# The down product of a SwiGLU block by Strassen's seven products, with the combinations of h formed in the gate and up tiles

## What is computed

```python
h = _rmsnorm(x, norm2_g)
ff = silu(einsum('btd,df->btf', h, w_gate)) * einsum('btd,df->btf', h, w_up)
return x + einsum('btf,fd->btd', ff, w_down)
```

## Time and profile before

| | us |
|---|---|
| median of 3 runs | 2161.58 (2156.37 to 2165.09) |
| the profiled execution | 2164.21 |
| its span | 2162.4 |
| TensorE busy | 2122.7 (98%) |
| gate and up tiles | about 1454 to 1898 |
| down product | about 1898 to 2154 |

### The profile page before, as it was taken

One profiled execution on the slowest core, in us unless ns is written; L12 is line 12 of the kernel. 1 busy time (PEld: TensorE's weight loads), 2 busy tenths in 40 slices (PEclk: granted clock), 3 DMA queues, 4 the chain that ended last, 5 costly groups with the idle time before them and its releaser, 6 DMA issues.

```text
span 2162.4 us, 36192 instructions
## 1 busy us (share of the span) xinstructions
PE 2122.7 (98%) x14248; PEld 1981.8 (92%) x14248; DVE 1070.9 (50%) x2112; ACT 632.3 (29%) x1354; POOL 723.7 (33%) x636
## 2 busy tenths in 40 slices
PE   7999999999999999999999999999999999999999
PEld 6788899999877778999989999999999999999998
DVE  5565777775233331333266544498554554452222
ACT  5221365535233232333221011133232322221001
POOL 3423320232212222222042434324444444554310
PEclk9999999999999999999999999999999999999999
DMA  6625534454548744555457551414545545387612
GB/s 196 211 84 190 175 108 148 134 183 164 184 152 296 263 139 148 163 149 161 119 194 264 181 175 61 152 62 159 202 143 179 186 147 178 105 326 291 258 44 79
DMA packets 233736, 365.17 MB, mean 169 GB/s; under 512 B 39223, under 2 KB 134263, under 8 KB 230871
## 3 DMA queue, kind: packets, MB, share of 16 engines
q1 hardware_dynamic: 211534, 317.48, 44.3%
q10 hardware_dynamic: 22032, 45.38, 6.0%
HBM read 276.19 MB, written 174.68 MB: 209 GB/s over the span
## 4 chain that ended last, share of the span: by engine, by line
PE 55%; DVE 4%; issue 1%; DMA 1%; ACT 0%; DVEq 0%; ACTq 0%
PE ps L2855 24%; PE ps L2199 17%; PE ps L366 4%; PE ps L367 4%; PE ps L368 4%; PE ps L1637 1%; DMA h_mem<-c_ht 1%; PE ps L1412 0%; DVE x_c L2549 0%; DVE x_a L2549 0%; PE ps L1629 0%; PE ps L1620 0%; PE ps L1646 0%; PE ps L3498 0%; DMA rw<-hm_t 0%
## 5 line engine op out<-in xcount | busy, mean ns | idle before, releaser
L341 POOL CAST whi<-raw 128x512 fp32r<-128x512 f32 x228 | 174.6, 766 | 1048.1 <-PE ps L682 429.4
L343 POOL TENSOR_TENSOR wlo<-raw,whi 128x512 fp32r<-128x512 f32 x231 | 323.7, 1401 | 31.6 <-issue 7.8
L366 PE MATMUL ps<-whi,x_a 128*128 128x512 f32 x416 | 179.4, 431 | 0.0
L736 ACT ACTIVATE zt<-ps 128x512 f32<-128x512 f32 x104 | 62.1, 597 | 362.1 <-PE ps L368 309.9
L368 PE MATMUL ps<-whi,x_a 128*128 128x512 f32 x416 | 167.4, 402 | 0.0
L367 PE MATMUL ps<-wlo,x_a 128*128 128x512 f32 x416 | 167.3, 402 | 0.0
L366 PE MATMUL ps<-whi,x_b 128*128 128x512 f32 x416 | 166.2, 399 | 0.0
L368 PE MATMUL ps<-whi,x_b 128*128 128x512 f32 x416 | 165.9, 399 | 0.0
L367 PE MATMUL ps<-wlo,x_b 128*128 128x512 f32 x416 | 165.9, 399 | 0.0
L2855 PE MATMUL ps<-x_a,whi 128*128 128x258 f32 x960 | 155.1, 283 | 2.5 <-DVE acc L2657 1.8
L2855 PE MATMUL ps<-x_c,whi 128*128 128x258 f32 x960 | 154.4, 283 | 0.5 <-DVE acc L3344 0.5
(11 more groups left out here) (416 smaller groups left out, 4944.4 us busy)
## 6 DMA issues: line engine op xcount, KB each, us to landing
out<-in_cache_kv_w SPq DMA_DIRECT2D x144, 512.0 KB, 6.4
raw<-in_w_in SPq DMA_DIRECT2D x147, 256.0 KB, 4.1
a_tr<-tt SPq DMA_DIRECT2D x48, 256.0 KB, 2.0
out<-in_cache_kv_w SPq DMA_DIRECT2D x24, 508.0 KB, 5.7
raw<-in_w_down SPq DMA_DIRECT2D x44, 256.0 KB, 6.1
gates<-e_sg ACTq DMA_DIRECT2D x16, 516.0 KB, 3.7
rw<-gates ACTq DMA_DIRECT2D x16, 516.0 KB, 4.9
out<-zt SPq DMA_DIRECT2D x26, 256.0 KB
```

The lines of the kernel that those rows point to most:

```text
L341: pool.tensor_copy(self.whi[:, self.place(p), :], raw).then_inc(self.w_hi, 1)
L343: pool.tensor_tensor(self.wlo[:, self.place(p), :], raw, self.whi[:, self.place(p), :].bitcast(F32), ALU.subtract).then_inc(self.w_lo, 1)
L366: nc.tensor.matmul(out, lhs[0], rhs[0], start=start, stop=False)
L736: act.activation(self.zt[:, u % Z, :], ps[:, u % 2, :], ACT.Copy, scale=self.scale(u)).then_inc(self.ev, 1)
```

## The change

The down product uses the same seven-product scheme. Hidden channels are taken in 11 pairs of tiles (2j, 2j + 1), tokens in two halves, and the 1024 outputs in two halves of four blocks. There are 16 further tiles, c = 22 to 37: tile c belongs to chunk n and output block m with (n, m) = divmod(c - 22, 4), and gives output blocks m and m + 4. The chunks are 3, 3, 3 and 2 pairs, so a tile is 7 products of 3 (or 2) blocks, 126 (or 84) matmuls of 258 columns. The raw weights of a tile are four slices of `w_down`, 128 x 384 (or 256), with runs of 512 bytes; their sums, roundings and rests are made as for gate and up, on the same engines and in the same ring. `load_pieces` and `split_weights` no longer handle `w_down`.

The seven left operands are h11, h21, h22 and four combinations. VectorE forms the combinations in the gate and up tiles (`dve_tees`: one subtraction after an even tile, three operations after an odd one), and SyncE stores them (`flush`, after the tile that follows began). `h_ff` holds 7 x 11 half rows. For this ha and hb have two places each, taken from the part of `acc` where raw weights landed; raw weights have one landing area left, and `load(c + 2)` waits until the fourth weight sum and the third weight rest of tile c + 1 are made.

In the down stage a "group" (n, i) is the half rows of chunk n for the i-th product of the sequence. There are 8 places of 6 half rows. `load_group` waits until the place is free (for chunks after the first: until product i - 1 of the chunk's fourth tile is done). ScalarE rounds it (`act_group`), VectorE takes the rests of groups 0, 1, 3, 5, 6 and GpSimd those of 2 and 4 (`group_rest`). The transposes of the end come in pairs in the last three tiles, into banks 6, 7 and 4, 5, which products 7 and 5 also use.

```diff
 PRODS = 7
-HELD = TILES * PRODS
-DOWN = 2 * TILES
+ALL = TILES + 16
...
 
-    return [range(0, 6), range(6, 12), range(12, 18), range(18, TILES)]
+    return [range(0, 3), range(3, 6), range(6, 9), range(9, TILES // 2)]
...
-        self.h_ff = dram("h_ff", (TILES, P, T))
+        self.h_ff = dram("h_ff", (PRODS, TILES // 2, P, HT))
...
+        rows = lambda a, half: [a[:, r, half * HT:(half + 1) * HT] for r in range(a.shape[1])]
+        areas = ((rw[:], products.rw32[:]), (flat(xa), flat(core.x_a32)), (flat(xc), flat(products.x_c32)), (low[:], low32[:]))
+        order = ((0, 0), (0, 1), (1, 0), (2, 1), (1, 1), (3, 0), (3, 1), (2, 0))
+        self.units = [u for a, half in order for u in rows(areas[a][0], half)]
+        self.units32 = [u for a, half in order for u in rows(areas[a][1], half)]
+        self.freed = [1, 6, 7, 7, 5, 2, 3, 3]
+        self.pq = self.spare[:, 0:HT]
+        self.has, self.hbs = [self.spare[:, HT:T], acc[:, 4, HT:T]], [acc[:, 5, 0:HT], acc[:, 5, HT:T]]
+        self.ts = [acc[:, 6, HT:T], acc[:, 7, HT:T]]
...
         else:
-            sp.wait_ge(core.a_lo, self.made(0 if c == 1 else c - 2, MAKE[-1]))
-        bank = self.raw_bank(c)[0]
+            sp.wait_ge(core.a_lo, self.made(c - 1, MAKE[2]))
...
         for x, name, h in ((1, "w_gate", 0), (2, "w_gate", 1), (4, "w_up", 1), (5, "w_up", 0)):
-            src = core.t[name].rearrange("(h k p) c -> h p k c", h=2, p=P)[h][:, :, c * P:(c + 1) * P]
-            sp.dma_start(self.raw_of(c, x).rearrange("p (k c) -> p k c", k=4), src).then_inc(
-                self.raw_in[bank], 16)
+            if c < TILES:
+                src = core.t[name].rearrange("(h k p) c -> h p k c", h=2, p=P)[h][:, :, c * P:(c + 1) * P]
+            else:
+                n, m = self.part_of(c)
+                at, pairs = (m if x < 4 else m + 4) * P, self.chunks[n]
+                src = core.t["w_down"].rearrange("(j h p) c -> h p j c", h=2, p=P)[h][:, pairs.start:pairs.stop, at:at + P]
+            sp.dma_start(self.raw_of(c, x).rearrange("p (k c) -> p k c", c=P), src).then_inc(self.raw_in, 16)
 
     def source(self, c, x):
 
 
...
+        for c in range(ALL):
...
-                at = self.ring(c, x)
-                pool.tensor_tensor(core.wlo[:, at, :], self.source(c, x), core.whi[:, at, :].bitcast(F32),
+                at, w = self.ring(c, x), self.width(c)
+                pool.tensor_tensor(core.wlo[:, at, 0:w], self.source(c, x), core.whi[:, at, 0:w].bitcast(F32),
                                    ALU.subtract).then_inc(core.a_lo, 1)
+            if c >= TILES and self.part_of(c)[1] == 0:
+                for i in self.POOLS:
+                    self.group_rest(pool, self.part_of(c)[0], i)
...
+        n, m = self.part_of(c)
+        if c >= TILES:
+            his, los = self.group(n, self.sequence(c).index(x))
+        for k in range(4 if c < TILES else len(self.chunks[n])):
+            if c >= TILES and m == 0:
+                self.wait_rest(pe, n, self.sequence(c).index(x), k)
...
+        if c == TILES - 1:
+            for x in MAKE[:6]:
+                self.act_round(c + 1, x)
+            self.act_group(0, 0)
+            self.act_group(0, 1)
+            self.act_round(c + 1, MAKE[6])
...
         self.wait_sum(act, c, "c11")
-        act.activation(self.ha, self.ha, ACT.Silu).then_inc(self.taken, 1)
+        act.activation(self.has[c % 2], self.has[c % 2], ACT.Silu).then_inc(self.taken, 1)
         if c == TILES - 1:
-            for e in range(2, 6):
-                self.act_row(e)
+            for i in (2, 3, 4):
+                self.act_group(0, i)
...
+        if c == TILES - 1:
+            self.act_group(0, 5)
+            self.act_group(0, 6)
+
+    def act_down(self, c):
+
+
+        n, m = self.part_of(c)
+        self.act_p1(c)
+        if n == len(self.chunks) - 1 and m:
+            self.act_turned(2 * m - 2)
+            self.act_turned(2 * m - 1)
+        if m == 0 and n:
+            self.act_group(n, 5)
+            self.act_group(n, 6)
+        if c + 1 < ALL:
+            for x in MAKE[:6]:
+                self.act_round(c + 1, x)
+            if m == 3:
+                self.act_group(n + 1, 1)
+            self.act_round(c + 1, MAKE[6])
+        if m == 2 and n + 1 < len(self.chunks):
+            self.act_group(n + 1, 0)
+        elif m == 3 and n + 1 < len(self.chunks):
+            for i in range(2, 5):
+                self.act_group(n + 1, i)
 
     def dve_last(self, c):
 
...
+    def dve_tees(self, c):
+
+
+        dve, (j, odd) = self.core.nc.vector, divmod(c, 2)
+        (h11, h21), (h12, h22), (t1, t4) = self.has, self.hbs, self.ts
+        self.wait_sum(dve, c, "hb")
+        if odd == 0:
+            dve.wait_ge(self.t_out[0], 16 * j)
+            dve.tensor_tensor(t1, h12, h11, ALU.subtract).then_inc(self.teed, 1)
+            return
+        dve.wait_ge(self.teed, 4 * j + 1)
+        dve.tensor_tensor(h12, h22, h12, ALU.subtract).then_inc(self.teed, 1)
+        dve.wait_ge(self.teed, 4 * j + 2)
+        dve.wait_ge(self.ha_out[0], 32 * j + 16)
+        dve.tensor_tensor(h11, h12, h11, ALU.add).then_inc(self.teed, 1)
+        dve.wait_ge(self.teed, 4 * j + 3)
+        dve.wait_ge(self.t_out[1], 16 * j)
+        dve.tensor_tensor(t4, h21, h11, ALU.subtract).then_inc(self.teed, 1)
 
...
+    def dve_down(self, c):
+
+
+        dve, acc = self.core.nc.vector, self.acc
+        (n, m), last = self.part_of(c), len(self.chunks) - 1
+        cu, c2, hb = self.rs[:, 0:HT], self.rs[:, HT:T], self.spare[:, HT:T]
+        more = c + 1 < ALL
+        if more:
+            self.dve_sums(c + 1, 0, 2)
+        self.dve_q(c)
+        if n == last and m:
+            self.dve_turned(2 * m - 2)
+            self.dve_turned(2 * m - 1)
+        if more:
+            self.dve_sums(c + 1, 2, 3)
+        if m == 0:
+            self.dve_group(n, 5)
+            if n:
+                self.dve_group(n, 6)
+        self.done(dve, c, 7)
+        self.wait_sum(dve, c, "q")
+        dve.tensor_tensor(half2(c2), half2(self.pq), self.bank(c, 7), ALU.add).then_inc(self.summed, 1)
+        if m == 0 and n == 0:
+            self.dve_group(n, 6)
+        self.done(dve, c, 5)
+        self.wait_sum(dve, c, "a")
+        dve.tensor_tensor(half2(c2), half2(c2), self.bank(c, 5), ALU.add).then_inc(self.summed, 1)
+        if more:
+            self.dve_sums(c + 1, 3, 4)
+        if m >= 2 and n < last:
+            self.dve_group(n + 1, m - 2)
+        self.done(dve, c, 2)
+        dve.wait_ge(self.products.x_in[m // 2], 64)
+        part = half2(acc[:, m, 0:HT])
+        dve.tensor_tensor(part, part, self.bank(c, 1), ALU.add).then_inc(self.summed, 1)
+        if m == 3 and n < last:
+            self.dve_group(n + 1, 3)
+        self.done(dve, c, 4)
+        dve.tensor_tensor(half2(cu), half2(self.pq), self.bank(c, 4), ALU.add).then_inc(self.summed, 1)
+        self.done(dve, c, 3)
+        if c == TILES:
+            dve.wait_ge(self.ha_out[0], 16 * TILES)
+        dve.tensor_tensor(half2(hb), half2(self.pq), self.bank(c, 3), ALU.add).then_inc(self.summed, 1)
+        self.wait_sum(dve, c, "c12")
+        part = acc[:, m, HT:T]
+        dve.tensor_tensor(part, part, hb, ALU.add).then_inc(self.summed, 1)
+        dve.wait_ge(self.products.x_in[m // 2 + 2], 64)
+        self.wait_sum(dve, c, "c21")
...
+    def flush(self, c):
+
+
+        sp, h, (j, odd) = self.core.nc.sync, self.core.h_ff, divmod(c, 2)
+        if odd == 0:
+            sp.wait_ge(self.teed, 4 * j + 1)
+            sp.dma_start(h[5 - 1, j], self.ts[0]).then_inc(self.t_out[0], 16)
+            return
+        self.wait_sum(sp, c, "hb")
+        sp.dma_start(h[3 - 1, j], self.hbs[1]).then_inc(self.hb_out[1], 16)
+        sp.wait_ge(self.teed, 4 * j + 2)
+        sp.dma_start(h[7 - 1, j], self.hbs[0]).then_inc(self.hb_out[0], 16)
+        sp.wait_ge(self.teed, 4 * j + 3)
+        sp.dma_start(h[6 - 1, j], self.has[0]).then_inc(self.ha_out[0], 16)
+        sp.wait_ge(self.teed, 4 * j + 4)
+        sp.dma_start(h[4 - 1, j], self.ts[1]).then_inc(self.t_out[1], 16)
...
-        if c + 2 < TILES:
-            self.load(c + 2)
+        if c:
+            self.flush(c - 1)
+        if c == TILES - 1:
+            for i in range(5):
+                self.load_group(0, i)
+        self.load(c + 2)
         core.copy_until(COPIES[0] + (COPIES[1] - COPIES[0]) * min(c + 1, TILES - 3) // (TILES - 3))
+        self.wait_sum(sp, c, "ha")
+        sp.dma_start(core.h_ff[c % 2, c // 2], self.has[c % 2]).then_inc(self.ha_out[c % 2], 16)
         if c == TILES - 1:
-            for e in range(2):
...
-            core.load_pieces(core.last + RAW)
-        elif c == TILES - 1:
+            self.load_group(0, 5)
             self.done(sp, c, 4)
             for k in range(4):
                 self.load_sum(k)
-            core.load_weights(core.last + 7)
-        self.wait_sum(sp, c, "hb")
-        sp.dma_start(core.h_ff[c, :, HT:T], self.hb).then_inc(self.hb_out, 16)
```

(80 more changed lines are left out.)

311 lines of the change are left out of this document (128 added, 183 removed).

## The result

The changed kernel takes 2202.0 us (median of 4 executions, 2193.4 to 2210.8) against 2159.3 for the kernel before on the same chip: 1.9% slower, ratio 1.0194, 95% interval 1.0145 to 1.0244. Forecast was 2149.1. The profiled execution took 2198.8 us, span 2196.9.

The account below looks back on a forecast made before the run. TensorE's matmuls, busy 98% of the span, were taken as the bound. -23.6 - 1.5 (today's down-stage waits) + 0.3 + 8.5 + 1.8 + 2.0 = -12.5 us; median 2161.6 becomes 2149.1, range 2144 to 2155, with rivals 2141 to 2162.

Parts of the forecast that it names:

- Count and price of the matmuls: Down product: 1584 matmuls at 155.0 ns become 1848 at 120.1 ns, 245.5 to 221.9 us, minus 23.6 us.
- The chunk changes: Down stage, where a new chunk's groups load: 0.3 us each at second and third change, 1.2 at the last, plus 1.8.
- VectorE has its rests at 24.5 and a at 25.2: Chunk change, us in a tile's own time: group 6's rests, then sum a, ready before product 4 asks at 25.9.
- every chunk change stalls: Rival, 18%: group 6 lands at 24.5, a comes at 29; 4.8 us at each of three changes, 2161.7 us.
- no copies run beside these loads: Chunk changes: the argument held against the late landings of 9.0 us seen for h under load.
- The handover: Tiles 21 to 22, gate and up to down: late group 6 delays copy p1, then VectorE's chain; plus 8.5 us.
- the low clock: Handover: idleness lowers TensorE's clock, 1.7 us lost, but hidden because products 2 and 4 wait for VectorE anyway.
- The gate and up tiles: VectorE's added combinations and the single weight landing area cost 0.3 us, in the second and third tile.
- The last tiles: Last three tiles: product 7 waits for VectorE's copy from the bank shared with transposes, 3 x 0.65, plus 2.0 us.
- The first rival: No handover wait to speak of, 14%: group 6 lands by 30, p1 at 32.4; loss 3 to 5, 2144 to 2146 us.

Follow-up runs that it names:

- e1: The changed kernel with the down stage's cache copies all issued by the thirteenth of its sixteen tiles, none in the last three: 2187.2 us.
- e10: The changed kernel with cache copies spread, VectorE's and ScalarE's work reordered, all rests of h on VectorE and neighbouring half rows' rests merged: 2151.8 us.
- e12: The same kernel as e10, repeated with more rounds: 1.6 us above its expected 2150 to 2153 us; with e10, 0.3 to 0.4% below the kernel before.

## Why the prediction was wrong

- **Count and price of the matmuls: right.** 118.3 ns where nothing waits (forecast 120.1).
- **The cause missed: VectorE's prices.** Every rest, combination and SBUF sum went into the sum at the 0.6 to 0.7 us of the earlier trace rows, the price where GpSimd is not in the way. At a chunk change GpSimd has seven weight rests and six rests of h, and VectorE's cost up to 1.8. The change added to just that: 11 half rows in each of seven groups need 77 rests, 55 of them VectorE's, where 22 row blocks had 22 of twice the width, and each can wait for GpSimd by itself.
- **The chunk changes: 1.8 us forecast, 21.0 measured**, and 2.7, 1.1 and 2.1 of low clock. The failed step is "VectorE has its rests at 24.5 and a at 25.2". On that same clock, where TensorE asks for a at 25.9 (1982.2 in the trace), the first change has its rests at 33.5 and a at 34.1. The landings were in time: ScalarE had cast group 6 by 1980.7, at 24.4 where 22.3 was forecast, and 2.2 us ahead of VectorE's first rest of group 5. The rival "every chunk change stalls" had the place but a late transfer as its cause, and half the size (14.4 us against 26.9). What was held against it, "no copies run beside these loads", is not so: SyncE issues three at 1953.1 and three at 1973.7.
- **The handover: +8.5 forecast.** Product 3 starts at 1922.8, 48.3 us after the start of tile 21, where 41.7 was forecast and 33.15 was due, and tile 22 as a whole takes 31.1 us (1894.75 to 1925.87) where 15.1 is its price: +16.0 in place of +8.5. The order of waits was right (ScalarE in group 6's cast, p1 behind it, then VectorE). The copy p1 ended at 38.6 and not 35.4: ScalarE began to cast group 6 at 36.4, where its landing was forecast for 33.0. One part of that is the store of ha, behind which SyncE issues groups 5 and 6: it went out at 22.9 and not 21.0, since the VectorE instruction ahead of it took 1.61 us and not 0.70. VectorE's chain from p1 to c22 took 9.4 us and not 6.3, its six rests 6.6 us instead of 3.7. And the low clock was not hidden throughout, as the forecast had it: product 3's 18 matmuls take 3.0 us and not 2.2.
- **The gate and up tiles: +0.3 forecast, +6.7 measured.** In tiles 3 to 20 nothing waits, as forecast (2497 matmuls in 300 us). In tile 2 three combinations take 1.67 us each ahead of q and a, because GpSimd's weight rests begin at the same landing: 3.7 us, and 2.8 of low clock behind it.
- **The last tiles: +2.0 forecast**, 1.7 in e1 (three of 0.56). But the cache copies, which I had not followed through the new `sp_down`, cost 16.0. That is a step omitted: a queue that is no longer held back by loads runs ahead of its neighbours' stores.
- The sum of it: beyond the forecast stand 25 us at the changes with their clock, 18 for the copies (16.2 and 2.8 of clock, less the 0.56 that was due), 7.5 at the handover and 6.4 in gate and up. They are 57, which is what lies between -12.5 and +44.5; the parts are each good to a us or so. e1 gives the copies 16.0, its waits and low clock at the changes being 2 us longer.
- e10's stretch is 10.5 us below before's (9.5 in e12). That this is close to the forecast of -12.5 is luck, as its waits are others than those of the forecast's sum. What it shows is that the matmuls do give something, when the rest is put right. As first measured, the change gave it back four times over.
- The first rival has a slip in its own sum: with p1 at 32.4 and the forecast's chain of 6.3 the loss is 5.5, not 3 to 5. Nothing measured came near it.

Not tried: whether either kernel gains from moving some of GpSimd's weight rests to VectorE (the kernel before has all its rests of h there already), and whether weight rests in wider pieces would free VectorE further.

## What to carry to other kernels

Before pricing an elementwise instruction, ask where its inputs lie and what GpSimd does at that moment: take its price from a row beside a working GpSimd if both inputs are in SBUF. Ask for the most and not for the median: here the median had 0.69 us and the most 1.79. Splitting one such instruction into several can cost a wait for each. And when a change takes loads out of an engine's queue, follow what else that queue issues: copies that were paced by the loads come out in one burst ahead of the stores that matter.
